# A hybrid-attention and mixture-of-experts layer on one core: an earlier first gather, two reordered steps of attention, and the experts' second product in halves

## The reference, cut to what matters

```
for l in range(DEPTH):                       # DEPTH = 1
    h = _rmsnorm(x, norm_attn[l])
    proj = h @ w_in[l]
    ...
    o_a = _nsa_mixer(...)                    # 8 heads: compressed, selected and window branch, gated
    o_b = _fox_mixer(...)                    # 4 heads with a forget-gate bias
    o_c = _diff_mixer(...)                   # 4 heads: difference of two softmax maps
    x = x + jnp.concatenate([o_a, o_b, o_c], axis=-1) @ w_out[l]
    x = x + _hier_moe(_rmsnorm(x, norm_ffn[l]), ...)
return _rmsnorm(x, norm_final)

# in _hier_moe, gate being zero for all but two of a token's experts:
for e in range(N_EXPERTS):                   # 32 experts
    a = hf @ w_e_gate[e]                     # 1024 x 256
    u = hf @ w_e_up[e]                       # 1024 x 256
    out = out + (jax.nn.silu(a) * u * gate[:, e:e + 1]) @ w_e_down[e]   # 256 x 1024
```

## Time and profile before

| | us |
|---|---|
| median of the timed runs | 1219.35 |
| the profiled execution | 1231.86 |
| its span, first to last instruction | 1230.1 |
| PE busy in the span | 1107.8 (90%) |
| DVE, ACT, POOL busy | 596.7, 382.3, 211.4 |
| mean granted clock of PE | 0.950 |

### The profile page before, as it was taken

One profiled execution on the slowest core, in us unless ns is written; L12 is line 12 of the kernel. 1 busy time (PEld: TensorE's weight loads), 2 busy tenths in 40 slices (PEclk: granted clock), 3 DMA queues, 4 the chain that ended last, 5 costly groups with the idle time before them and its releaser, 6 DMA issues.

```text
span 1230.1 us, 29634 instructions
## 1 busy us (share of the span) xinstructions
PE 1107.8 (90%) x12090; PEld 903.3 (73%) x12090; DVE 596.7 (49%) x1584; ACT 382.3 (31%) x693; POOL 211.4 (17%) x460
## 2 busy tenths in 40 slices
PE   5999899999899999999899899948999999999910
PEld 5989788778688888888777688847777777776700
DVE  5341344225466666665685434464344433333428
ACT  6411112222355555544677122200111111111103
POOL 1020000000333233221374000010001000000040
PEclk9999899999799999999999899967999999999965
DMA  9021744362557878764321422277999999999464
GB/s 350 18 86 37 271 149 151 139 187 98 126 113 182 208 204 219 196 147 95 106 62 28 155 95 96 79 279 260 379 378 376 406 374 369 387 384 371 188 238 198
DMA packets 69430, 251.59 MB, mean 205 GB/s; under 512 B 22224, under 2 KB 30320, under 8 KB 59440
## 3 DMA queue, kind: packets, MB, share of 16 engines
q1 hardware_dynamic: 59376, 219.54, 53.5%
q0 software_dynamic: 6112, 16.79, 4.0%
q10 hardware_dynamic: 3808, 13.37, 2.9%
HBM read 205.34 MB, written 49.15 MB: 207 GB/s over the span
## 4 chain that ended last, share of the span: by engine, by line
PE 72%; DMA 12%; DVE 7%; issue 4%; SPq 2%; ACT 1%; POOL 1%; DVEq 1%; POOLq 0%; ACTq 0%
PE PS L2145 13%; PE PS L1826 12%; PE PS L2002 8%; PE PS L2153 8%; PE PS L2082 8%; PE PS L1815 5%; DMA wdn<-in_wdn 5%; PE PS L1980 4%; PE PS L1941 3%; PE PS L1981 3%; DMA k<-T_d 3%; PE PS L2136 2%; DVE x L1772 1%; SPq L620 1%; DMA wst<-in_wt 1%
## 5 line engine op out<-in xcount | busy, mean ns | idle before, releaser
L2145 PEld LDWEIGHTS PS<-XT,wgu 128*64 128x64 f32 x4352 | 185.3, 139 | 31.6 <-issue 30.6
L1088 ACT ACTIVATE pt<-PS,cst 128x512 f32<-128x512 f32 (+3 forms) x288 | 168.0, 652 | 115.4 <-PE PS L1981 88.2
L2145 PE MATMUL PS<-XT,wgu 128*64 128x96 f32 x4352 | 191.4, 250 | 5.8 <-issue 2.7
L1396 DVE CUSTOM_DVE_ANT_0 junkm<-PS,cst 128x512 f32<-128x512 f32 (+3 forms) x276 | 133.5, 531 | 86.9 <-PE PS L1941 85.1
L2002 PEld LDWEIGHTS PS<-V,pt 128*64 128x64 f32 x3840 | 122.4, 138 | 22.5 <-issue 9.5
L2002 PE MATMUL PS<-V,pt 128*64 128x65 f32 x3840 | 137.9, 226 | 0.1
L2153 PE MATMUL PS<-wdn,aT 128*96 128x512 f32 x272 | 122.7, 593 | 1.6 <-DVE YO L1720 0.9
L1826 PE MATMUL PS<-hTh,wth 128*128 128x512 f32 x256 | 102.9, 402 | 5.0 <-DVE wtl L1243 5.0
L1826 PE MATMUL PS<-hTh,wtl 128*128 128x512 f32 x256 | 100.7, 393 | 0.0
L1826 PE MATMUL PS<-hTl,wth 128*128 128x512 f32 x256 | 100.7, 393 | 0.0
L821 POOL TENSOR_SCALAR_AFFINE_SELECT pt<-pt 128x128 f32<-128x128 f32 x224 | 64.6, 294 | 164.4 <-ACT pt L1088 121.2
(11 more groups left out here) (275 smaller groups left out, 1630.9 us busy)
## 6 DMA issues: line engine op xcount, KB each, us to landing
wgu<-in_wgu SPq DMA_DIRECT2D x34, 2048.0 KB, 13.8
wdn<-in_wdn SPq DMA_DIRECT2D x34, 1024.0 KB, 21.1
q<-T_d SPq DMA_DIRECT2D x58, 256.0 KB, 4.2
k<-T_d SPq DMA_DIRECT2D x58, 256.0 KB, 5.4
Y_d<-YO ACTq DMA_DIRECT2D x34, 384.0 KB, 10.0
wst<-in_wt SPq DMA_DIRECT2D x16, 512.0 KB, 7.0
T_d<-thi SPq DMA_DIRECT2D x16, 512.0 KB, 2.6
T_d<-tlo SPq DMA_DIRECT2D x16, 512.0 KB, 3.9
```

Of the source, the lines that this page charges most:

```text
L1088: ins = nc.scalar.activation(pt[:, (n + 2) % 6, 0:nt * P], PS[:, n % 3, 0:nt * P], ACT.Exp, scale=C("slopes", h, h + 1), bias=C("kb", w, w ...
L1396: V_.tensor_tensor_reduce(out=junk_[:, 0:L], in0=PS[:, bank, 0:L], in1=tab, scale=1.0, scalar=-3e38, op0=ALU.add, op1=ALU.max, accum_out=m ...
L2145: ins = mm(PS[h * HD:(h + 1) * HD, 2 + p, f * CAP:(f + 1) * CAP], wgu[q][:, c, lo:lo + HD], XT[:, p, c, :], start=(c == 0 and f == 0), sto ...
```

## The change

It has four parts.

1. Attention, start. SP issues the shift row of `full[1]` before the load of `full[3]`, not behind it, and no longer waits for `full[2]` before that load. The Q1 and K1 transfers of `full[2]` count on a semaphore of their own (`lx_in`), so that its maxima wait for four transfers and not for six.
2. Attention, end. The first half of the first tile's transposes goes ahead of the last products with V on PE, and DVE's `o_lo` of it ahead of the last batch of outputs.
3. Experts, start. SP waits for the first gather (`xg_in[0]`) before it loads experts 2 and 3, not before expert 4 alone.
4. Experts, second product. It becomes three fp32r products of halves. ACT rounds `wdn` to `wdnh` (one buffer for all experts) and the activations to `aTh`, DVE subtracts to get `wdnl` (in `wdn`'s own place) and `aTl`. The loads of `wgu` and `wdn` count on semaphores of their own: up(n) waits for `wgu` alone, and the split of `wdn` waits for `wdn` and, since `wdnh` is a single buffer, for down(n-1).

```
@@ SP, attention
-            sp_.wait_ge(ld_in[PLAN.full[2].set], 96)
-            load_unit(PLAN.full[3])
...
+                if f == 1:
+                    load_unit(PLAN.full[3])
@@ SP, experts
-                sp_.dma_start(wgu[q][:], ...).then_inc(we_in[q], 16)
-                sp_.dma_start(wdn[q][:], ...).then_inc(we_in[q], 16)
+                sp_.dma_start(wgu[q][:], ...).then_inc(wu_in[q], 16)
+                sp_.dma_start(wdn[q][:], ...).then_inc(wd_in[q], 16)
...
             load_expert(1, 1)
+            sp_.wait_ge(xg_in[0], 16)
             load_expert(2, 2)
             sp_.wait_ge(h_lg, 8)
             load_expert(3, 3)
             sp_.wait_ge(dve_did, DV.of("ids_ov"))
-            sp_.wait_ge(xg_in[0], 16)
             load_expert(4, 4)
@@ ACT, experts
+            def wd_high(n):
+                act.wait_ge(wd_in[n % RING], 16 * (n // RING + 1))
+                if n:
+                    act.wait_ge(m_dn, n)
+                for c in range(2):
+                    copy(wdnh[:, c, :], wdn[n % RING][:, c, :]).then_inc(wd_hi, 1)
+            def a_part(n):
+                act.wait_ge(m_prod, n + 1)
+                if n >= 2:
+                    act.wait_ge(m_dn, n - 1)
+                copy(aTh[:, n % 2].rearrange("p c t -> p (c t)"), gd[:]).then_inc(m_ah, 1)
             for n in range(NB):
                 m_exp(n)
                 if n + 1 < NB:
                     m_x(n + 1)
+                a_part(n)
                 if n:
                     m_out(n - 1)
+                wd_high(n)
@@ DVE, end of attention
             for slot_ in SLOTS:
+                if slot_ == LAST + 1:
+                    o_lo(0, 0, (0,))
...
-            o_lo(0, 0, (0,))
@@ DVE, experts
-                V_.tensor_tensor(out=aT[...], in0=gd[:], in1=up, op=ALU.mult).then_inc(m_act, 1)
+                V_.tensor_tensor(out=gd[:], in0=gd[:], in1=up, op=ALU.mult).then_inc(m_prod, 1)
+            def a_rest(n):
+                dve.wait_ge(m_ah, n + 1)
+                V_.tensor_tensor(out=flat_(aTl), in0=gd[:], in1=flat_(aTh).bitcast(f32), op=ALU.subtract)\
+                  .then_inc(m_act, 1)
+            def wd_low(n):
+                for c in range(2):
+                    dve.wait_ge(wd_hi, 2 * n + c + 1)
+                    V_.tensor_tensor(out=wdnl[n % RING][:, c, :], in0=wdn[n % RING][:, c, :],
+                                     in1=wdnh[:, c, :].bitcast(f32), op=ALU.subtract).then_inc(wd_lo, 1)
@@ PE
+                elif k == 0 and x is PLAN.full[2]:
+                    pe_.wait_ge(lx_in, 64)
...
-            pe_.wait_ge(o_free, PLAN.batches)
+                if slot_ == LAST:
+                    o_transposes(0, (0,))
                 for x, k in PLAN.s_at.get(slot_ - PLAN.DEEP, ()):
                     values(x, k)
...
-                        ins = mm(PS[0:CAP, 5 + h, :], aT[:, p, c, :], wdn[q][:, c, h * 512:(h + 1) * 512],
-                                 start=(c == 0), stop=(c == 1))
+                        for x, w in ((aTh, wdnh), (aTl, wdnh), (aTh, wdnl[q])):
+                            ins = mm(PS[0:CAP, 5 + h, :], x[:, p, c, :], w[:, c, h * 512:(h + 1) * 512],
+                                     start=(c == 0 and x is aTh and w is wdnh), stop=(c == 1 and w is wdnl[q]))
...
             def m_down(n):
                 pe_.wait_ge(m_act, n + 1)
+                pe_.wait_ge(wd_lo, 2 * n + 2)
```

More of the change, by code:

```diff
@@ L356, in program @@
         gd = at("gd", [P, 2 * CAP], f32, ZE + 25 * KB)
-        aT = at("aT", [P, 2, 2, CAP], f32, ZE + 26 * KB)
+        aTh, aTl = (at(n, [P, 2, 2, CAP], f32r, ZE + 26 * KB + 1536 * k) for k, n in enumerate(("aTh", "aTl")))
+        aT = at("aT", [P, 2, CAP], f32, ZE + 26 * KB)
+        TABLES = (4 * COL["dist"][0] + 31) // 32 * 32
+        assert TABLES + 8 * KB <= 4 * COL["distc"][1]
+        wdnh = at("wdnh", [P, 2, D], f32r, TABLES)
         wgu = [at(f"wgu{q}", [P, KC, 2 * DE], f32, o)
                for q, o in enumerate((ZE + 8 * KB, ZD, ZD + 24 * KB, ZB + 32 * KB, ZC))]
-        wdn = [at(f"wdn{q}", [P, 2, D], f32, o)
-               for q, o in enumerate((ZE, ZD + 16 * KB, ZD + 40 * KB, ZB + 48 * KB, ZC + 16 * KB))]
+        wdn, wdnl = ([at(f"{n}{q}", [P, 2, D], dt, o)
+                      for q, o in enumerate((ZE, ZD + 16 * KB, ZD + 40 * KB, ZB + 48 * KB, ZC + 16 * KB))]
+                     for n, dt in (("wdn", f32), ("wdnl", f32r)))
         y1 = at("y1", [P, NT, D], f32, ZD)
@@ L462, in program @@
         h_st = [sem(f"h_st{p}") for p in range(2)]
-        we_in = [sem(f"we_in{q}") for q in range(RING)]
+        wu_in = [sem(f"wu_in{q}") for q in range(RING)]
+        wd_in = [sem(f"wd_in{q}") for q in range(RING)]
+        wd_hi = sem("wd_hi")
+        wd_lo = sem("wd_lo")
+        m_prod = sem("m_prod")
+        m_ah = sem("m_ah")
         xg_zero = sem("xg_zero")
@@ L619, in load_unit @@
                                             (Q2, 0, 0, q0), (K2, 0, 1, k0))[4 * (x.n == 2):]:
-                    sp_.dma_start(dst[x.set][HD * half:HD * half + HD, :].bitcast(f32), T_r[part, r0:r0 + HD, :])\
-                       .then_inc(ld_in[x.set], 16)
+                    ins = sp_.dma_start(dst[x.set][HD * half:HD * half + HD, :].bitcast(f32), T_r[part, r0:r0 + HD, :])
+                    ins.then_inc(lx_in if x is PLAN.full[2] and dst in (Q1, K1) else ld_in[x.set], 16)
             def shift_row(x):
@@ L690, in load_expert @@
             def load_expert(e, q):
[L691 to L692 removed]
+                sp_.dma_start(wgu[q][:], a["wgu"][e].rearrange("p (k n) -> p k n", k=KC)).then_inc(wu_in[q], 16)
+                sp_.dma_start(wdn[q][:], a["wdn"][e].rearrange("p (k n) -> p k n", k=2)).then_inc(wd_in[q], 16)
             sp_.wait_ge(pv_done, PLAN.pieces)
@@ L1505, in _, with o_lo @@
             t_lo(15, 1, (1,))
+            def o_lo(t, p, halves=(0, 1)):
+                for c in halves:
+                    dve.wait_ge(g_hi, 2 * t + c + 1)
+                    V_.tensor_tensor(out=otl[:, p, 4 * c:4 * c + 4, :].rearrange("p k t -> p (k t)"),
+                                     in0=PS[:, c, :],
+                                     in1=oth[:, p, 4 * c:4 * c + 4, :].rearrange("p k t -> p (k t)").bitcast(f32),
+                                     op=ALU.subtract).then_inc(g_lo, 1)
             for slot_ in SLOTS:
+                if slot_ == LAST + 1:
+                    o_lo(0, 0, (0,))
                 for x, c in PLAN.out_at.get(slot_, ()):
@@ L1517, in _ @@
                     shift_rows(x)
-            def o_lo(t, p, halves=(0, 1)):
-                for c in halves:
-                    dve.wait_ge(g_hi, 2 * t + c + 1)
-                    V_.tensor_tensor(out=otl[:, p, 4 * c:4 * c + 4, :].rearrange("p k t -> p (k t)"),
-                                     in0=PS[:, c, :],
-                                     in1=oth[:, p, 4 * c:4 * c + 4, :].rearrange("p k t -> p (k t)").bitcast(f32),
-                                     op=ALU.subtract).then_inc(g_lo, 1)
-            o_lo(0, 0, (0,))
             dve.wait_ge(rs_done, RS_D + 1)
@@ L1906, in loaded @@
                 f = PLAN.full.index(x)
-                return 96 * ((f - 1) // 3 + 1) - 64 * (x.set == 0) if f else 96
+                return 96 * ((f - 1) // 3 + 1) - 64 * (x.set < 2) if f else 96
             def operands(x):
@@ L1960, in scores @@
                     pe_.wait_ge(aug_set[s], 2)
-                    if x.n == 2:
+                    if x in PLAN.full[1:3]:
                         pe_.wait_ge(ld_in[s], loaded(x))
@@ L2045, in o_transposes @@
                     ins.then_inc(g_tr, 1)
+            for slot_ in SLOTS:
+                for x, k in PLAN.s_at.get(slot_, ()):
+                    scores(x, k)
+                for x, k in PLAN.m_at.get(slot_, ()):
+                    max_pass(x, k)
+                for x in PLAN.tp_at.get(slot_, ()):
+                    shift_T(x)
+                if slot_ == LAST:
+                    o_transposes(0, (0,))
+                for x, k in PLAN.s_at.get(slot_ - PLAN.DEEP, ()):
+                    values(x, k)
             def h_transposes(t):
@@ L2152, in down_product, with down_plain @@
                     for c in range(2):
-                        ins = mm(PS[0:CAP, 5 + h, :], aT[:, p, c, :], wdn[q][:, c, h * 512:(h + 1) * 512],
+                        for x, w in ((aTh, wdnh), (aTl, wdnh), (aTh, wdnl[q])):
+                            ins = mm(PS[0:CAP, 5 + h, :], x[:, p, c, :], w[:, c, h * 512:(h + 1) * 512],
+                                     start=(c == 0 and x is aTh and w is wdnh), stop=(c == 1 and w is wdnl[q]))
+                return ins
+            def down_plain():
+                for h in range(2):
+                    for c in range(2):
+                        ins = mm(PS[0:CAP, 5 + h, :], aT[:, c, :], wdn[0][:, c, h * 512:(h + 1) * 512],
                                  start=(c == 0), stop=(c == 1))
```

32 lines of the change are left out of this document (14 added, 18 removed).

## The result

| | before | after |
|---|---|---|
| median of the timed runs | 1221.73 (7 runs) | 1214.24 (7 runs, 1206.0 to 1218.3) |
| the profiled execution | 1231.86 | 1214.73 |
| its span | 1230.1 | 1213.0 |

The ratio is 0.993, with a 95% interval from 0.990 to 0.996: 7.5 us faster, where 18.0 was forecast. 1214 lies outside the forecast range. The two profiled executions differ by 17.1 us. That is near the 18.0 of the forecast by chance, as the experiments show.

What follows compares the result with a forecast made beforehand. PE was taken to bound attention, and DMA the experts' stage at 10.26 us a block. Gains of 10.5 (attention start), 0.5 (attention end) and 7.0 (experts) made 18.0: 1219.35 to 1201 us, range 1188 to 1212 (own range 1194 to 1208).

Steps and rivals of the forecast that it cites:

- the 18.0: Whole kernel: total gain in us, 10.5 + 0.5 + 7.0, carried unscaled from the profiled execution to the median.
- Start of attention: First units of attention: waits of 1.26 and 3.22 us go and the clock stays full; 10.5 us gained.
- End of attention: From the last V product to `project`: starts 2.8 us earlier, then a 2.5 us wait; 0.5 us gained.
- Start of the experts: First gather lands sooner: up(0) 4.1 us earlier, expert 5's load 4.9 us earlier.
- the saturated stretch: Experts' blocks with DMA always busy: starts 4.9 us earlier, then 28 blocks at 10.26 us as before.
- The second product: Experts' down product: 2.75 us instead of 3.53, a PE block 8.9 us, later about 1.4 us wait per block.
- Rival 4: Experts' blocks: the split does not fit beside the up product; 1204 to 1206 us, strong form about 1219 (3%).
- The tail: Last expert block: the split waits for down(32), 5.0 to 5.5 us, then 2.8 us of product; end at 1168.
- The experts' 7.0 us: Whole experts' stage: its end at 1168 against 1174.85, 7.0 us less in all, bounds 4.0 and 10.
- rivals, 1: Experts' loads: DMA in timed runs is faster than in the profiled one; 1188 us, chance 17%.
- Rival 3: Attention: it keeps its waits or the clock falls anyway, gaining 0 to 4.5 us; 1207 to 1212, chance 8%.
- Rival 2: Experts' stage: the clock falls at each block's wait for `wgu`; 1275 us at the lower level throughout, slow form 6%.

Runs made afterwards that it cites:

- the second profile: The kernel before, unchanged, profiled once more: 1222.44 us, 9.4 us less than its first profile.

## Why the prediction was wrong, step by step

One measure takes in the gather and the blocks: from the first gather's issue to the end of the last product, by the profiles' timelines, in us (counts of profiles in brackets).

| | plain second product | split | split, last block plain |
|---|---|---|---|
| gather as before | 353.2 to 354.8 (4) | 353.2 (1) | 347.5 (1) |
| gather ahead | 352.2 to 354.5 (3) | 350.4 to 352.8 (4) | 344.4 to 347.0 (3) |

What the split does in there can be read off two distances, in the profiles with full loads. Up(33) starts 338.6 to 341.2 us after the gather's issue with the plain second product (seven profiles), and 331.2 to 334.4 with the split (nine): some 7 us earlier. From there to the end of the last product it is 13.6 us with the plain product, 18.5 to 19.6 with the split, and 13.2 where the last block alone is plain. So the split gains, and the last block spends nearly all of it. The gain has a bound. With the plain product up(33) starts 3.2 to 7.1 us after the last `wdn` has landed, with the split between 1.0 us ahead of it and 0.8 behind: PE has caught up with the loads, and can't pass them.

- *Start of attention, 10.5 us.* The mechanism is right: both waits are gone and the clock stays up. The size was read from the worst of three profiles. Alone it measured 8.3 us by the medians (ratio 0.992 to 0.996, so 5 to 10), inside the bounds of 4.5 to 10.7.
- *End of attention, 0.5 us.* The 2.8 us and the 2.5 us wait came as told, without a clock spell behind the wait. The prediction reckoned with a new spell there, and not with the one of 6.8 us that was there and is gone. From the last V product to the first gather the profiles have 141.4 to 144.0 us with the old end and 139.9 to 143.2 with the new: a gain of about 1.5. Some 0.6 us of it are the transposes, which now lie ahead of the last V product, so that about 0.9 is left, inside the bounds. Both parts of attention together measured 9.3 of the 11.0 us.
- *Start of the experts, 4.1 us at up(0) and 4.9 us at expert 5's load.* Both came (4.0 and 5.0 us, counted from the gather's issue), and here is the first step that failed: "the saturated stretch starts 4.9 us earlier". I had the queue busy with loads 2 to 4 until the ring's next load was due, and did not draw the conclusion. A stretch that is fed without a gap starts with load 2, and load 2 is issued 4.4 us behind the gather (812.89 against 808.45), where it was 11.5 us ahead of it. So expert 5's `wdn` lands 0.7 us earlier and not 4.9, the last one 2.5, and for the gather alone the table has 0.4 us.
- *The second product.* A block of 9.0 us on PE came (forecast 8.9), but PE waited for `wgu` in four blocks and not in each of the last twenty or so, and lost somewhat more in the gaps that nothing names. Up(33) came 6.4 us earlier where the forecast has 1161.2 - 1152.1 = 9.1. The split fits: it is done 4.8 us after up(5) starts, and 5.6 after up(33) (forecast 5.5). Rival 4 falls.
- *The tail.* It is the larger of the two shortfalls in the experts' stage: from up(33) to the end 19.4 us, where the forecast has 1168 - 1152.1 = 15.9 and the kernel before 13.6. The wait was right at 5.56 us. The product behind it ran at a clock of 0.54 and took 5.2 us instead of 2.8. I had weighed the clock for the blocks, but not for the longest wait of all. This is 2.4 us of the 3.5; a plain last product gives 5.6.
- *The final stage.* It has no step in the prediction. In the kernel after with quick turns the change made 19 empty turns of a loop longer by 3.8 us, of which 2 reach the end, and 8 where the turns are long. This is the second step that failed: whatever is not in the diff was taken to be as long as before.
- *From the profile to the median.* I saw that the profiled execution was 12.5 us above the median and carried the 18.0 over unscaled. The profiled execution of before had long turns (5.5 us), while its timed runs, 1219 to 1223 us, are where the second profile with quick turns lies.

In all, 9.3 for attention, about 2 for the gather and the split, less 2 for the turns, give 9, against 7.5 (5 to 12) measured. The experts' 7.0 us is the term that failed: about 0 in place of 7.

Of the rivals, 1 is excluded: the second profile of before, at 1222.44 us as long as the timed runs, has 10.32 us from landing to landing, and the first one 10.25. The transfers are not faster there. Rival 3's number, 1207 to 1212, came closest, which is luck: its condition, that attention keeps its waits, did not hold. Rival 2 fell. PE waited for weights up to 2.5 us at a time, and the clock was 0.99 over the stage. The Trainium skill, TensorE: Matmul & The Clock Gate, section HAM oscillation, has a kernel whose clock fell with a DMA wait in every tile. Its waits are longer than those of PE between blocks here, so it doesn't bear out rival 2 as the prediction had it. Here the clock stayed up behind nearly all waits of 1.5 to 2.5 us in the experts' stage, and fell with the one of 5.56.

## What to carry to other kernels

When a stretch is fed by transfers without a gap, find the first transfer from which on there is none: only what starts that one earlier, or cuts bytes, moves it as a whole. Compute saved inside it is worth about what the engine trails the last landing by, so read that distance first, and look at the last block for what nothing covers. Take a second profile of the kernel before pricing stalls from one, and compare stage by stage. Look at the control flow that runs while nothing else does: an empty loop costs its turns.

## What the runs showed of the hardware

- An empty turn of a loop (compare, branch, count) took 0.53 us on DVE in all profiles of kernels without the split and 0.72 us in all with it, as far as the turns were quick, though the loop's source was the same but for one operand. Why was not tried.
- In the first profile of before and in all four on the second chip, single instructions of DVE's sequencer took 0.70 us each, for the last 9 to 16 us of the loop, while the gathers ran. That the second chip's medians for the kernel before are 6 to 9 us higher than on the others fits it, but what sets it off is open.
- A wait of 5.5 us was followed by a last product at a clock of 0.50 to 0.67, 4.3 to 5.4 us long, in all six profiles in which the last block is split; behind a wait of 0.9 us the plain one ran at 1.00 in 3.65 us, in all twelve profiles that have it.
- With the split and full loads PE had gaps of 0.5 to 2.2 us in the middle of a product, where no semaphore stands: 10.1 us in all from 867 to 1150 us in the first profile of after, 0.7 us in the first of before. Some come at the same record in several profiles (22 records ahead of the first product's end in all three profiles of after and in that of the split alone). What makes them is open.
